# A row norm folded through the product that reads it, and the weight splits moved into the convolution chain

## The reference, cut to what matters

```python
# end of the first block
new_xs = xs + gate[:, None] * y            # y = (...) @ w_out
x = _rmsnorm(new_xs, final_g)              # x / sqrt(mean(x*x)) * final_g, per row
# start of the second block
proj = x @ w_in                            # 2048 x 10304
z, xbc, dt = jnp.split(proj, [4096, 10240], -1)
xbc = silu(causal_depthwise_conv(xbc, conv_w, conv_b))   # 4 taps over the tokens
dt = softplus(dt + dt_bias)
...
y = y * silu(z)                            # gate of the scan's output
x = layer_norm(ALPHA * x + h, ...)         # the normed rows are needed here too
```

## Time and profile before

| | value |
|---|---|
| median of 3 runs | 2096.57 us (2094.46 to 2097.85) |
| the profiled execution's own time | 2094.8 us |
| its span, first to last instruction | 2093.0 us |
| mean granted TensorE clock | 0.990 of full |
| busy share: TensorE, VectorE, ScalarE, POOL | 97%, 64%, 50%, 3% |
| chain that ended last | TensorE 91%, VectorE 4%, ScalarE 2%, DMA 2% |

### The profile page before, as it was taken

One profiled execution on the slowest core, in us unless ns is written; L12 is line 12 of the kernel. 1 busy time (PEld: TensorE's weight loads), 2 busy tenths in 40 slices (PEclk: granted clock), 3 DMA queues, 4 the chain that ended last, 5 costly groups with the idle time before them and its releaser, 6 DMA issues.

```text
span 2093.0 us, 30992 instructions
## 1 busy us (share of the span) xinstructions
PE 2035.8 (97%) x12236; PEld 1770.6 (85%) x12236; DVE 1339.2 (64%) x1775; ACT 1052.7 (50%) x1504; POOL 71.0 (3%) x80
## 2 busy tenths in 40 slices
PE   6999999999999999999999999999899999999998
PEld 4568888688899879999998888888799889998786
DVE  5447655477766556666776666666774755775555
ACT  4235555444434343444566666666555445775432
POOL 0001200000000000000001000000000000000000
PEclk9999999999999999999999999999999999999999
DMA  8785522367764653355454455545354454324552
GB/s 346 304 327 200 182 101 104 118 241 281 286 231 170 228 193 130 146 198 176 169 200 174 169 195 196 190 181 201 134 185 177 162 183 178 120 103 160 188 194 101
DMA packets 57658, 393.57 MB, mean 188 GB/s; under 512 B 6635, under 2 KB 9083, under 8 KB 10571
## 3 DMA queue, kind: packets, MB, share of 16 engines
q1 hardware_dynamic: 54240, 376.07, 48.9%
q0 software_dynamic: 2304, 14.49, 1.8%
q10 hardware_dynamic: 1008, 1.53, 0.2%
HBM read 389.89 MB, written 2.16 MB: 187 GB/s over the span
## 4 chain that ended last, share of the span: by engine, by line
PE 91%; DVE 4%; ACT 2%; DMA 2%; issue 1%; DVEq 0%; SPq 0%; ACTq 0%
PE ps L2200 13%; PE ps L2202 13%; PE ps L2201 13%; PE ps L2220 10%; PE ps L2212 9%; PE ps L2214 9%; PE ps L2213 9%; PE ps L2221 5%; PE ps L2305 1%; DMA raw<-in_tiles 1%; PE ps L2453 1%; PE ps L2431 1%; PE ps L2290 1%; PE ps L2643 1%; PE ps L2642 1%
## 5 line engine op out<-in xcount | busy, mean ns | idle before, releaser
L1146 DVE TENSOR_TENSOR w_lo<-raw,w_hi 128x1024 fp32r<-128x1024 f32 (+1 forms) x612 | 743.5, 1227 | 506.4 <-ACT w_hi L489 504.8
L489 ACT ACTIVATE w_hi<-raw 128x1024 fp32r<-128x1024 f32 (+1 forms) x612 | 638.3, 1052 | 616.0 <-PE ps L2202 301.7
L2212 PE MATMUL ps<-act,w_hi 128*128 128x256 f32 x1152 | 333.2, 289 | 2.0 <-DVE w_lo L1146 1.2
L2214 PE MATMUL ps<-act,w_lo 128*128 128x256 f32 x1152 | 326.9, 284 | 0.0
L2213 PE MATMUL ps<-act,w_hi 128*128 128x256 f32 x1152 | 326.8, 284 | 0.0
L2220 PE MATMUL ps<-act,w_hi 128*128 128x512 f32 x896 | 315.2, 397 | 1.3 <-DVE side L1430 1.3
L2200 PE MATMUL ps<-w_hi,act 128*128 128x512 f32 (+1 forms) x640 | 255.1, 399 | 2.9 <-DVE act L1189 2.9
L2221 PE MATMUL ps<-act,w_lo 128*128 128x256 f32 x896 | 250.2, 279 | 0.0
L2202 PE MATMUL ps<-w_hi,act 128*128 128x512 f32 (+1 forms) x640 | 248.6, 388 | 0.0
L2201 PE MATMUL ps<-w_lo,act 128*128 128x512 f32 (+1 forms) x640 | 247.9, 387 | 0.0
L2200 PE MATMUL ps<-w_hi,gated 128*128 128x512 f32 x576 | 227.2, 394 | 2.3 <-DVE gated L1970 1.4
(11 more groups left out here) (328 smaller groups left out, 2730.6 us busy)
## 6 DMA issues: line engine op xcount, KB each, us to landing
raw<-in_tiles SPq DMA_DIRECT2D x350, 1024.0 KB, 4.8
gatedf<-acs_dram POOLq DMA_DIRECT2D x8, 1024.0 KB, 7.3
raw<-in_tiles SPq DMA_DIRECT2D x4, 672.0 KB, 4.5
x<-in_x SPq DMA_DIRECT2D x2, 1024.0 KB, 6.5
side<-in_ctx SPq DMA_DIRECT2D x2, 1024.0 KB, 11.0
side<-in_ln_g POOLq DMA_DIRECT2D x2, 1024.0 KB, 6.6
out_dram<-x SPq DMA_DIRECT2D x8, 256.0 KB, 2.7
side<-in_b_ada POOLq DMA_DIRECT2D x1, 1024.0 KB, 4.6
```

The lines of the kernel that those rows point to most:

```text
L489: e.activation(w_hi[:, nth(u) % SPLIT, :, :w], raw[:, t % RAW, 2 * h:2 * h + 2, :w], ACT.Copy).then_inc(hi_done, 1)
L1146: e.tensor_tensor(w_lo[:, slot, :, :w], raw[:, t % RAW, 2 * h:2 * h + 2, :w], w_hi[:, slot, :, :w].bitcast(F32), ALU.subtract).then_inc(lo ...
L2212: e.matmul(o, wh, hi, start=first and f % 2 == 0, stop=False, skip_group_check=True)
L2214: ins = e.matmul(o, wl, hi, start=False, stop=last and f % 2 == 1, skip_group_check=True)
```

## The change

The row norm's factor is no longer applied before the product. In four parts:

1. **Turns move into "out".** The unscaled rows are turned a quarter at a time in the middle of out's blocks 1, 2 and 3; the fourth quarter is turned after two units of ssd_x's block 0. The gain `final_g` is a per-partition column there and is multiplied in by four ScalarE and four VectorE operations a quarter (`out_high`, `out_low`), which take the place of `high_x` and `low_x`. Three quarters go to `gated` and are later copied to `act`: the high parts by ScalarE (`high_copy`), the low parts by POOL, ahead of POOL's four small loads.
2. **A row of factors.** VectorE scales the identity by the two columns of factors, TensorE multiplies by ones (two fp32 products of 128 columns, in block 0 of ssd_x), VectorE copies the result to `rstd_row`.
3. **The factor behind the products.** `conv` starts with two products of a PSUM bank with `rstd_row`, for all 12 blocks; the `dt` product is scaled once; `z_silu` takes the factor as its scale. `rms_piece` still makes the normed rows, now behind the convolutions of blocks 0 and 1.
4. **Order of the splits.** VectorE splits units 8b+12 and 8b+13 inside the convolution, after its second and third groups of four; ScalarE splits them ahead of silu instead of behind it.

Cut here: `final_g` joins the columns of `vec`; `out_squares` writes its unused output elsewhere; `high_x`, `high_and_splits`, `low_x`, `normed_and_splits` are removed; `z_silu` gets `scale=`; `dt_read` waits for the scaling of `dt`; `layer_scaled` and `layer_rows` wait for one more turn.

```diff
+            def out_high(b):
+                e.wait_ge(S["x2_turned"], b + 1)
+                for c in range(4):
+                    ins = e.activation((act if b == 3 else gated)[:, 0, 4 * b + c, :],
+                                       ps[:, 4 + 2 * (b % 2) + c // 2, (c % 2) * 256:(c % 2) * 256 + 256], ACT.Copy,
+                                       scale=vec[:, V_FG + 4 * b + c:V_FG + 4 * b + c + 1])
+                ins.then_inc(S["x2_hi"], 1)
+
+            def high_copy(q):
+                e.wait_ge(units_used, ready("out", 3))
+                e.activation(act[:, 0, 4 * q:4 * q + 4, :], gated[:, 0, 4 * q:4 * q + 4, :].bitcast(F32),
+                             ACT.Copy).then_inc(S["x2_hi"], 1)
+            u0 = 2 * FIRST["out"]
+            for b in range(4):
+                splits(u0 + 8 * b + 4, 4)
+                if b:
+                    out_high(b - 1)
+                splits(u0 + 8 * b + 8, 4)
+                if b == 1:
                     sqrt_table()
-                out_squares(b, k)
-
-            segment("out", 4, 4, out_squares_table)
+                out_squares(b, b % 2)
+            u0 = 2 * FIRST["ssd_x"]
+            splits(u0 + 4, 1)
             root(sm[:, 40:42], sm[:, 36:38], S["row_mean"], 3, S["row_root"])
...
+            out_high(3)
+            splits(u0 + 5, 1)
+            high_copy(0)
+            splits(u0 + 6, 1)
+            high_copy(1)
+            splits(u0 + 7, 1)
+            high_copy(2)
...
                     if k or not isinstance(i, int):
-                        splits(ahead, 4, i, 16)
+                        splits(ahead + 2, 2, i, 16)
                     else:
-                        high_and_splits(ahead - 4, S["x2_turned"], S["x2_hi"])
                         dt_high()
                     if k and isinstance(i, int):
                         dt_read()
                     if k or not isinstance(i, int):
                         x_tokens(b - 1, (k + 1) % 2)
-                    splits(ahead + 4, 4, i, 16)
+                    splits(ahead + 4, 6, i, 16)
+                    if isinstance(i, int) and k == 0:
+                        e.wait_ge(S["x2_copied"], 3)
                     conv_silu(gatedf[:, LO + k * 1024:LO + (k + 1) * 1024], 0, b)
             each(e, 4, conv_x)
...
                 if b == 0:
-                    splits(ahead, 4)
+                    splits(ahead + 2, 2)
                     x_tokens(7, 1)
...
+                    e.wait_ge(S["normed2"], 8)
                     e.activation(x[:, :, :], x[:, :, :], ACT.Copy, scale=ALPHA).then_inc(S["x_scaled"], 1)
...
+            def out_low(b):
...
+                for c in range(4):
+                    ins = e.scalar_tensor_tensor(out=r[:, 1, 4 * b + c, :],
...
+                                                 in1=r[:, 0, 4 * b + c, :].bitcast(F32), op0=ALU.mult, op1=ALU.subtract)
+                ins.then_inc(S["x2_lo"], 1)
             splits(u0 + 4, 8)
             add_bias()
             out_add(0, 0)
-            splits(u0 + 12, 8)
-            out_add(1, 1)
-            splits(u0 + 20, 8)
-            out_add(2, 0)
-            splits(u0 + 28, 6)
-            out_add(3, 1)
-
+            for b in range(1, 4):
+                splits(u0 + 8 * b + 4, 4)
+                out_low(b - 1)
+                splits(u0 + 8 * b + 8, 3 if b == 3 else 4)
+                out_add(b, b % 2)
+            u0 = 2 * FIRST["ssd_x"]
+            splits(u0 + 3, 2)
             e.wait_ge(S["sq2"], 8)
...
-            e.reciprocal(sm[:, 44:46], sm[:, 40:42]).then_inc(S["vec_step"], 1)
+            e.reciprocal(sm[:, 92:94], sm[:, 40:42]).then_inc(S["vec_step"], 1)
             e.wait_ge(S["vec_step"], VEC_STEPS + 12 + 1)
-            e.wait_ge(S["final_loaded"], 16)
+            for n in range(2):
+                e.tensor_scalar(t1[:, n * P:(n + 1) * P], ident, sm[:, 92 + n:93 + n], None, ALU.mult).then_inc(S["vec_step"], 1)
+            out_low(3)
+            splits(u0 + 5, 3)
+            rstd_row = t0[:, 0:256]
+            e.wait_ge(S["x2_turned"], 5)
+            e.tensor_copy(rstd_row, ps[:, 4, 0:256]).then_inc(S["vec_step"], 1)
+            e.wait_ge(S["vec_step"], VEC_STEPS + 12 + 4)
...
             def conv(nb, ch0):
-                def go(b, k):
+                def go(b, k, u, i=0, step=0):
                     e.wait_ge(units_used, ready("ssd_x") + nb + b)
                     e.wait_ge(S["conv_silu"], 2 * nb + 2 * b)
-                    before = 14 * nb + 14 * b
+                    before = 16 * nb + 16 * b
+                    for j in range(2):
+                        v = ps[:, 2 * k + j, :].rearrange("p (c t) -> p c t", c=2)
+                        e.tensor_tensor(v, v, rstd_row.unsqueeze(1).to_broadcast([P, 2, 256]), ALU.mult).then_inc(S["conv_step"], 1)
...
+                        if s in (1, 2):
+                            splits(u + 11 + s, 1, i, step)
...
-            def x_block(b, k):
-                conv_x(b, k)
+            def x_block(b, k, u, i):
+                splits(u + (6 if k or not isinstance(i, int) else 8), 6 if k or not isinstance(i, int) else 4, i, 16)
+                conv_x(b, k, u, i, 16)
+                if isinstance(b, int) and b == 0:
+                    e.wait_ge(S["dt_mm"], 1)
+                    e.tensor_tensor(ps[0:64, 6, 0:256], ps[0:64, 6, 0:256], rstd_row[0:64, :], ALU.mult).then_inc(S["vec_step"], 1)
+                    rms_piece(0)
+                    rms_piece(1)
                 if isinstance(b, int) and b == 1:
                     dt_size()
+                    rms_piece(2)
+                    rms_piece(3)
             conv_x, conv_bc = conv(0, 0), conv(8, 32)
             dt_low()
-            segment("ssd_x", 4, 8, x_block, 4)
+
+            def x_blocks(i):
+                for k in range(2):
+                    x_block(2 * i + k, k, 2 * FIRST["ssd_x"] + 8 * k, i)
+            each(e, 4, x_blocks)
             for b in range(4):
-                early = 2 if b in (1, 2) else 0
                 ahead = 2 * FIRST["ssd_bc"] + 8 * b + 4
-                splits(ahead + early, 8 - early)
+                splits(ahead + 2, 6)
                 if b == 2:
                     e.wait_ge(S["dt_turned"], 1)
                     e.tensor_copy(t1[:, :], ps[:, 7, 0:256]).then_inc(S["dt_ready"], 1)
-                conv_bc(b, b % 2)
+                conv_bc(b, b % 2, ahead - 4)
                 if b == 0:
-                    splits(ahead + 8, 2)
                     dt_parts()
                 if b == 1:
-                    splits(ahead + 8, 2)
                     dt_sums()
...
-            splits(Z0 + 4, 2)
             weighted(0)
...
+            e.wait_ge(units_used, ready("out", 3))
+            e.wait_ge(S["x2_lo"], 3)
+            for q in range(3):
+                e.tensor_copy(act[:, 1, 4 * q:4 * q + 4, :], gated[:, 1, 4 * q:4 * q + 4, :].bitcast(F32)).then_inc(
+                    S["x2_copied"], 1)
             bc(t0[:, 384:448], a["ssd_d_skip_2"], S["rows_loaded"])
...
-            segment("out", 4, 4, out_block)
+
+            def turn_x(q):
+                e.wait_ge(S["out_step"], 2 * q + 2)
+                if q >= 2:
+                    e.wait_ge(S["x2_lo"], q - 1)
+                turn4(lambda c, tt: x[:, tt, c * P:(c + 1) * P], q, 4 + 2 * (q % 2)).then_inc(S["x2_turned"], 1)
+            pair_free(BI["out"])
+            for b in range(4):
+                u0 = 2 * FIRST["out"] + 8 * b
+                if b == 0:
+                    out_block(0, 0, 0, u0, 0)
+                    continue
+                pair_free(BI["out"] + b)
+                gemm(u0, 4, act, 2 * (b % 2), True, ends=False)
+                if b == 1:
+                    e.wait_ge(S["gate_ready"], 1)
+                turn_x(b - 1)
+                gemm(u0 + 4, 4, act, 2 * (b % 2), True, kc0=8, starts=False)
...
-                    e.wait_ge(S["gate_ready"], 1)
-                    normed_gemm(u0, False, S["normed2"], S["x2_lo"], S["x2_turned"])
+                    e.wait_ge(S["x2_lo"], 3)
+                    gemm(u0, 2, gated, 0, False, ends=False)
+                    turn_x(3)
+                    gemm(u0 + 2, 4, gated, 0, False, kc0=4, starts=False, ends=False)
+                    e.wait_ge(S["vec_step"], VEC_STEPS + 12 + 3)
+                    for n in range(2):
+                        ins = e.matmul(ps[:, 4, n * P:(n + 1) * P], tables[:, T_TRI + P:T_TRI + 2 * P], t1[:, n * P:(n + 1) * P],
+                                       start=True, stop=True)
+                    ins.then_inc(S["x2_turned"], 1)
+                    e.wait_ge(S["x2_lo"], 4)
+                    gemm(u0 + 6, 2, act, 0, False, kc0=12, starts=False)
                     return
                 gemm(u0, 4, act, 2 * k, False, i, step, ends=False)
                 turn_group(b - 1, (k + 1) % 2)
...
                 if k and isinstance(i, int):
+                    e.wait_ge(S["x2_hi"], 7)
+                    e.wait_ge(S["x2_copied"], 3)
```

(44 more changed lines are left out.)

20 lines of the change are left out of this document (7 added, 13 removed).

## The result

| | before | after |
|---|---|---|
| median of 12 runs, the two kernels in turn on the same chip | 2095.52 us (2092.04 to 2097.85) | 2099.55 us (2096.03 to 2100.57) |
| the profiled execution's own time | 2094.8 us | 2098.72 us |
| its span | 2093.0 us | 2097.0 us |
| mean granted TensorE clock | 0.990 | 0.992 |

The ratio is 1.0019 with an interval of 1.0011 to 1.0026: the changed kernel is some 4 us slower. That is inside the 0.2% that I had called no change and inside my range, but the interval leaves out zero, and my sum had said 0.2 us faster. The question is therefore why both large terms, each near 11 us, did not cancel.

What follows compares the result with a forecast made beforehand. TensorE, busy for 97% of the span, was taken as the bound. 2094.8 - 10.9 + 10.7 = 2094.6 for the profiled execution, 2096.4 us for the median; own range 2093.5 to 2100, eight in ten 2088 to 2102.

Steps and rivals of the forecast that it cites:

- both large terms: 10.9 us removed at the norm and block 0 of ssd_x; 10.7 us given back, mostly by late turns behind the convolutions.
- No gap at the norm, block 0 in 24.3: Between "out" and ssd_x: TensorE no longer waits for the row's factor, and block 0 takes 24.3 us.
- The cover that I named: Block 0's own stream hides the copies to `act` and POOL's queued loads, costed at nothing.
- The chain: VectorE's convolution ahead of silu: scalings 1.2 plus splits 2.3, 3.5 us later against 1.75 slack; turns 1.7 late, 10.7 in all.
- Its place behind the split of unit 15 does not change, so it stays.: First of eight turns, held by `dt_read`: its present wait of 1.6 us would stay the same.
- The removal: Norm gap and block 0: 37.6 us becomes 24.3, with 2.4 moved into "out"; 10.9 us removed, bounds 6.1 and 11.7.
- The chain is covered: Rival: lengthening ahead of silu stays under the slack, seven stalls vanish, 2084.2; half counted, near 2089. Chance 0.19, whole or half.
- The stalls cost the clock: Rival: new 1.7 us stalls at turns drop TensorE's clock, 4.7 us per fall; one gives 2101, three 2110. Chance 0.13.
- The norm's wait stays: Rival: a late split or part in block 0 only moves the gap, 2098 to 2103; shares 0.07 with a dearer chain.
- What the profile would show: Signs: block 0 in 24 to 25 us, clock 1.00, six or seven silu waits of 1.6 to 2, block period 25.6.

Runs made afterwards that it cites:

- with the splits behind: Changed kernel with VectorE's splits of units 8b+12 and 8b+13 behind the convolution, ScalarE's order kept: 2085.75 us, ratio 0.9951.
- the chain alone: Kernel before with only the new order of the splits on both engines, old norm, no scalings: 2098.21 us, ratio 1.0010.
- The version without scalings: Changed kernel without the two scalings by the row factor at the head of each convolution: 2089.94 us, ratio 0.9974.
- the old order: Changed kernel with the kernel before's order of splits on both engines, units 8b+12 and 8b+13 behind silu: 2093.49 us, ratio 0.9991.
- the seven executions: Profiled executions with the old norm, two of them from experiments; end of "out" to end of block 0: 35.5 us in three, 37.0 to 37.6 in four.
- the second comparison: Changed kernel measured once more without edit, against the kernel before: 2098.50 us (11 runs) against 2095.54 (23 runs), ratio 1.0011.

## Why the prediction was right or wrong

*No gap at the norm, block 0 in 24.3.* Right: from the end of "out" it takes 24.33 us, and the stretch above has 24.10 us of matmuls in 24.10. The cover that I named held; no row of block 0 waits for `w_lo`, a copy or a quarter. The three turns in "out" cost 2.7 and not 2.4 us (3.1 less the start-up's 0.4).

*The chain.* Right in every term: scalings 1.20 (taken 1.2, bounds 1.1 and 1.46), splits 2 x 1.13 (2.3), seven late turns 12.0 us and the last one's gain 1.4, against 6 x 1.7 = 10.3 and 1.7 - 1.45. A scaling, which writes into PSUM, takes the 0.69 us that `out_add` takes from PSUM to SBUF. That the two would take 2 x 0.69 is not borne out: two that last 0.69 each end within 1.29 us, so they start 0.60 apart.
The prediction took that price from one sentence of the Trainium skill (VectorE: DVE Perf Modes, "The DRAIN you can't avoid"). The same section goes on to say that a next operation that is not held starts earlier, and the trace agrees with that by these 0.60 us.

*"Its place behind the split of unit 15 does not change, so it stays."* This step failed: 1.60 became 2.29. Two things come together behind block 0. The first is the splits inside the convolution. The prediction took their high parts to be there; behind block 0 they are not, since unit 12's waits until TensorE has used unit 8, and the 5.5 us of dt_product stand before that. VectorE of the changed kernel stands idle in the middle of its convolution:

```profile
818.92 1.23 DVE L1159 TENSOR_TENSOR w_lo<-raw,w_hi 128x1024 fp32r<-128x1024 f32 x1 [2.59 <-ACT w_hi L490]
```

So this convolution ends at 824.5; with the splits behind it ends at 819.65. That alone does no harm: the chain alone on the kernel before has such a wait too (3.79 us) and leaves the first turn at 1.6. The second is on ScalarE. The chain alone:

```profile
831.27 1.28 ACT L749 ACT_TABLE_LOAD   x1
833.33 1.41 ACT L749 ACTIVATE gatedf<-tables 128x512 f32<-128x512 f32 x2 [0.77 <-DVE tables L1557]
```

The version without scalings, which has the changed kernel's 2.3:

```profile
824.86 1.28 ACT L760 ACT_TABLE_LOAD   x1 [2.11 <-DVE tables L1566]
826.15 1.15 ACT L760 ACTIVATE gatedf<-tables 128x512 f32<-128x512 f32 x2
827.21 1.99 ACT L490 ACTIVATE w_hi<-raw 128x1024 fp32r<-128x1024 f32 x2
829.11 0.45 ACT L779 ACTIVATE gatedf<-ps,sm 64x256 f32<-64x256 f32 x1
```

The load of silu's table used to run while ScalarE waited for the convolution. Now it starts only when the convolution is done, and pushes silu, two splits and `dt_read` back by 1.28 us, of which 0.7 reach the turn. This alone does no harm either. With the splits behind, the load is not covered (821.93, behind a split), nor is it in the old order (817.63, after 8.2 us of waiting for the convolution), but there the convolution ends early and the turn waits 1.6. In the source the difference ahead of the first silu is the wait for the three copies (`x2_copied`). In the changed kernel POOL had ended them at 793, so the wait itself was long over. That its place is what moved the load is read from the rows and the diff; it wasn't tried by itself.

*The removal, "37.6 - 24.3 - 2.4 = 10.9".* This is the term that was mis-sized, and the largest part of what was wrong in the sum. It took one execution's fall of the clock for the price. With the mean of the seven executions and the measured turns it is 36.5 - 24.3 - 2.7 = 9.5, and 8.5 to 10.5 by single executions. That is 1.4 less: 1.1 by the shorter falls, 0.3 by the dearer turns. With 0.7 at the first turn the sum would have been some 1.9 us slower and not 0.2 faster; the fall behind the first turn, 1.5 us in one of three executions of the changed kernel, adds 0.5 in the mean, and 0.15 is lost at 1107. The 2.6 us that come of this lie inside both measured intervals (about 2.3 to 5.4 us for the first comparison, 0.4 to 4.2 for the second), whose medians are 4.0 and 3.0; the rest is open.
The version with the splits behind prices the removal without the long chain. It is 9.8 us faster than before, where my terms give 10.9 + 1.45 = 12.35. Of these 2.5 us, 1.4 is again the removal and 0.6 the new wait for low parts at 1088, by the starts. The last 0.5 is open; the interval of that version reaches 2.8 us to either side, so its median alone would not have refuted the 12.35.
Two smaller slips of the prediction change nothing: with the products by ones hidden and the turns at 0.6 the upper bound of the removal is 11.9 and not 11.7, and half of the 3.5 us of chain would be all of the slack and make no turn late.

*The rivals.* "The chain is covered" is out as the change stands, and is what happens once the splits are moved: its 2084.2 is near the 2085.75 measured. "The stalls cost the clock" was right about the place and wrong about the waits: seven of 1.5 us never cost the clock in three profiled executions, the one of 2.3 did in two of four (the version without scalings counted), and a fall there was worth 1.5 us and not 4.7, since it lasted 3.4 us and not 10. "The norm's wait stays" is out: the time measured lies in its 2098 to 2103, but no matmul of block 0 waits.

*What the profile would show.* Turns inside "out", seven waits for silu (of 1.5 us by the view, where 1.6 to 2 were named), and no wait behind the last turn came true; the block period is 23.9 + 1.7. The clock of 1.00 up to 1000 came in two of three executions; the third had 0.66 over 830 to 835.

## What to carry to other kernels

Work that is "to be made anyhow" isn't free if it stands between a product's end and the signal that another engine will wait for: measure that consumer's slack (here 1.85 us) and put into the chain only what the consumer needs (1.20), the rest behind it. Half of a reordering can carry all of its gain: with the scalings in place the high parts ahead of silu on ScalarE were needed, and the low parts inside VectorE's chain cost 12.75 us. And a term that contains a fall of the clock is taken from several executions; one gave 10.9 where the mean of seven gives 9.5.

## What the runs showed of the hardware

The same gap of 6.09 us was followed by 6.8 us at half clock in three executions and by about 10 in four others, and the 3.5 us pause before y_product by 10.2 to 17.1. The seven waits of 1.5 us were followed by no fall, those of 2.3 and 2.4 by one of 3.4 us in three executions of five. At the norm this is a scatter of up to 2 us from execution to execution; with 11 runs against 23 the interval of the second comparison was still 1.9 us to either side.

A tiny VectorE operation was slowed while POOL copied. VectorE's timeline of the changed kernel, and POOL's:

```profile
791.19 0.82 DVE L1527 TENSOR_SCALAR sm<-sm 128x2 f32<-128x2 f32 x1
792.28 0.17 DVE L1529 RECIPROCAL sm<-sm 128x2 f32<-128x2 f32 x1 [0.27 <-ACT sm L519]
```

```profile
788.10 4.88 POOL L2171 CAST act<-gated 128x1024 fp32r<-128x1024 f32 x3 [70.18 <-DVE x L1502]
```

The same operation on two numbers a row takes 0.17 us in all seven executions with the old norm, where POOL copies nothing there, and 0.82 in all seven with the new one. It ended at 792.01, as POOL's second cast did (791.99), so it looks as if it had to wait for that cast. Not every operation is held up like this: the reciprocal ran inside the third cast (791.94 to 792.98) in 0.17. POOL's casts took 1.92 and 2.03 us beside VectorE's splits and 1.04 after them, and one of the splits 1.37 instead of 1.22. Why is not shown. Here it cost nothing, since the row of factors was not due before 803.
